# FFN up-projection on Trainium2: ten seven-product channel pairs per layer instead of seven, in groups of three

## The reference

```python
D_MODEL = 1024
SEQ = 512
D_FF = 2816
CONV_WIDTH = 3
...
def conv_ffn(x, w_up, conv_w, conv_b, w_down):
    h = x @ w_up
    ch = h.shape[-1]
    h = lax.conv_general_dilated(h, conv_w[:, None, :], window_strides=(1,), padding=((CONV_WIDTH - 1, 0),), dimension_numbers=('NWC', 'WIO', 'NWC'), feature_group_count=ch) + conv_b
    gate, val = jnp.split(h, 2, axis=-1)
    return (jax.nn.silu(gate) * val) @ w_down
...
        x = x + rms_norm(conv_ffn(rms_norm(x, pre_ffn), *ffns[i]), post_ffn)
```

## Time and profile before

| | |
|---|---|
| median of 3 runs | 2040.71 us (2038.3 to 2041.9) |
| the profiled execution | 2042.29 us, of which 2040.6 us are the span |
| PE busy | 2026.4 us (99%) |
| DVE, ACT, POOL busy | 79%, 55%, 21% |
| instructions | 33333 |
| PE clock granted | full throughout |

### The profile page before, as it was taken

One profiled execution on the slowest core, in us unless ns is written; L12 is line 12 of the kernel. 1 busy time (PEld: TensorE's weight loads), 2 busy tenths in 40 slices (PEclk: granted clock), 3 DMA queues, 4 the chain that ended last, 5 costly groups with the idle time before them and its releaser, 6 DMA issues.

```text
span 2040.6 us, 33333 instructions
## 1 busy us (share of the span) xinstructions
PE 2026.4 (99%) x12636; PEld 1750.7 (86%) x12636; DVE 1619.3 (79%) x2555; ACT 1115.0 (55%) x1861; POOL 433.7 (21%) x482
## 2 busy tenths in 40 slices
PE   9999999999999999999999999999999999999998
PEld 8889998888988899888877888998888889999887
DVE  6668878889467887899888669777997668877898
ACT  4755545447335555546656646555465755545555
POOL 0520332210000232120035402322110520332220
PEclk9999999999999999999999999999999999999999
DMA  8123344384432334467421123334674122334393
GB/s 291 64 104 125 109 130 150 121 255 172 145 129 75 97 105 129 145 190 243 166 73 42 63 83 104 119 104 155 197 237 163 65 104 83 109 122 147 115 269 122
DMA packets 82570, 276.42 MB, mean 135 GB/s; under 512 B 9408, under 2 KB 13632, under 8 KB 82032
## 3 DMA queue, kind: packets, MB, share of 16 engines
q1 hardware_dynamic: 59184, 214.67, 30.4%
q0 software_dynamic: 11200, 24.12, 5.8%
q10 hardware_dynamic: 12032, 35.54, 4.8%
HBM read 256.43 MB, written 14.73 MB: 133 GB/s over the span
## 4 chain that ended last, share of the span: by engine, by line
PE 91%; DVE 5%; DMA 2%; ACT 1%; issue 0%; DVEq 0%; ACTq 0%; SPq 0%
PE ps L2437 12%; PE ps L2438 12%; PE ps L2439 12%; PE ps L2649 6%; PE ps L3018 5%; PE ps L3019 5%; PE ps L3020 5%; PE ps L2976 5%; PE ps L2978 5%; PE ps L2977 5%; PE ps L2509 2%; PE ps L2465 2%; PE ps L2466 2%; PE ps L2467 2%; DMA raw<-slabs 2%; PE ps L2497 1%
## 5 line engine op out<-in xcount | busy, mean ns | idle before, releaser
L2437 PE MATMUL ps<-h_hi,w_hi 128*128 128x512 f32 (+1 forms) x1104 | 433.0, 392 | 0.0
L2438 PE MATMUL ps<-h_lo,w_hi 128*128 128x512 f32 (+1 forms) x1104 | 429.6, 389 | 0.0
L2439 PE MATMUL ps<-h_hi,w_lo 128*128 128x512 f32 (+1 forms) x1104 | 428.9, 389 | 0.0
L1603 DVE TENSOR_TENSOR w_lo<-raw,w_hi 128x1024 fp32r<-128x1024 f32 x300 | 372.0, 1247 | 39.1 <-ACT w_hi L901 35.5
L901 ACT ACTIVATE w_hi<-raw 128x1024 fp32r<-128x1024 f32 x312 | 326.4, 1053 | 133.1 <-DVE raw L2251 74.0
L2437 PEld LDWEIGHTS ps<-h_hi,w_hi 128*128 128x128 f32 x1104 | 207.6, 188 | 44.0 <-issue 4.0
L2439 PEld LDWEIGHTS ps<-h_hi,w_lo 128*128 128x128 f32 x1104 | 207.3, 188 | 43.2
L2438 PEld LDWEIGHTS ps<-h_lo,w_hi 128*128 128x128 f32 x1104 | 207.7, 188 | 38.9
L1281 ACT ACTIVATE work<-ps,conv_sb 128x512 f32<-128x512 f32 x120 | 93.0, 775 | 162.6 <-PE ps L2439 133.2
L3018 PE MATMUL ps<-w_hi,h_hi 128*128 128x512 f32 x408 | 159.7, 391 | 2.1 <-DVE w_lo L1603 2.1
L3020 PE MATMUL ps<-w_hi,h_lo 128*128 128x512 f32 x408 | 158.8, 389 | 0.0
(11 more groups left out here) (365 smaller groups left out, 5054.6 us busy)
## 6 DMA issues: line engine op xcount, KB each, us to landing
raw<-slabs SPq DMA_DIRECT2D x368, 512.0 KB, 4.1
act<-slabs POOLq DMA_DIRECT2D x64, 256.0 KB, 5.6
bias<-slabs SPq DMA_DIRECT2D x16, 512.0 KB, 6.3
x_dram<-x ACTq DMA_DIRECT2D x16, 512.0 KB, 5.0
x<-x_dram ACTq DMA_DIRECT2D x16, 512.0 KB, 4.9
raw<-act POOLq DMA_DIRECT2D x28, 256.0 KB, 3.3
act<-slabs SPq DMA_DIRECT2D x12, 512.0 KB, 5.4
bias_dram<-bias_rows ACTq DMA_DIRECT2D x2, 2048.0 KB, 12.3
```

The costliest lines, as they stand in the source:

```text
L1603: ve.tensor_tensor(w_lo[:, c % RING, :], raw[:, raw_slot(c), :], w_hi[:, c % RING, :].bitcast(f32), ALU.subtract).then_inc(lo_made, 1)
L2437: pe.matmul(ps[:, bank, cols], hi, h_hi[:, k, cols], start=k == 0, stop=False)
L2438: pe.matmul(ps[:, bank, cols], hi, h_lo[:, k, cols], start=False, stop=False)
L2439: last = pe.matmul(ps[:, bank, cols], lo, h_hi[:, k, cols], start=False, stop=k == KT - 1)
```

## The change

Pairs 4 to 17 are now: 4 fast, 5 ordinary, then three groups that start at `f` = 6, 10 and 14: `f`, `f + 1`, `f + 2` fast and `f + 3` ordinary. That is ten fast and four ordinary pairs a layer, instead of seven and seven. Inside a group PE interleaves products of neighbouring fast pairs. PSUM is shared out in four couples of banks, so a pair takes the banks of the pair four before. The orders of ACT, DVE, POOL and SP in this stretch are written anew as `first_period`, `period` and `last_period`; one instruction becomes four at the program's start (the negated convolution taps). The arithmetic of a fast or an ordinary pair is as before.

```diff
-FASTS = (FAST_END - FAST) // 2
+FAST_RUNS = 6, 10, 14
+IN_GROUP = 3
+FAST_PAIRS = [FAST] + [q + e for q in FAST_RUNS for e in range(IN_GROUP)]
+FASTS = len(FAST_PAIRS)
+X1_ORDER = [FAST] + [q + e for q in FAST_RUNS for e in (1, 0, 2)]
+UP_PRODUCTS = [(FAST, p) for p in (1, 2, 6, 4, 3)] + [
+    (q + e, p) for q in FAST_RUNS for e, p in (
+        (0, 1), (0, 2), (0, 6), (1, 1), (1, 2), (0, 4), (0, 3), (1, 6), (2, 1), (1, 4), (2, 2), (1, 3), (2, 6),
+        (2, 4), (2, 3))]
...
+        def part_count(L, q, name):
+
+            return FASTS * L + (X1_ORDER if name == "x1" else FAST_PAIRS).index(q) + 1
+
+        def product_count(L, q, p):
+
+            return len(UP_PRODUCTS) * L + UP_PRODUCTS.index((q, p)) + 1
...
-            return (0 if q // 2 % 2 else 4) + e
+            return 2 * ((q + 2) % 4 if FAST <= q < FAST_END else q % 2) + e
...
+                def load(q, e):
+
+                    c = up_slab(L, q, e)
+                    if q - 2 not in FAST_PAIRS:
+                        sp.wait_ge(lo_made, made(c - RAW))
+                    elif e:
+                        sp.wait_ge(part_lo_made["x3"], part_count(L, q - 2, "x3"))
+                        sp.wait_ge(part_lo_made["x4"], part_count(L, q - 2, "x4"))
+                    else:
+                        sp.wait_ge(part_lo_made["x1"], part_count(L, q - 2, "x1"))
+                        sp.wait_ge(up_x2, fast(L, q - 2) + 1)
+                        sp.wait_ge(up_x3, fast(L, q - 2) + 1)
+                    sp.dma_start(raw[:, raw_slot(c), :], slabs[dram(c)]).then_inc(raw_in[raw_slot(c)], 16)
+
+                def load_pair(q):
+
+                    load(q, 0)
+                    load(q, 1)
+
+                load_pair(FAST)
+                load_pair(FAST + 1)
+                for f in FAST_RUNS:
+                    load(f, 0)
+                    load(f + 1, 0)
+                    load(f, 1)
+                    load(f + 1, 1)
+                    load(f + 2, 0)
+                    load(f + 2, 1)
+                    load(f + 3, 0)
+                    load(f + 3, 1)
+                load_pair(FAST_END)
...
-                fourth_sum(L, FAST)
-                for j in range(STEPS - 1):
+                fourth_sum(L, 4)
+                fourth_sum(L, 6)
+                fourth_sum(L, 7)
+                down_sums(L, 0)
+                fourth_sum(L, 8)
+                down_sums(L, 1)
+                down_sums(L, 2)
+                fourth_sum(L, 10)
+                fourth_sum(L, 11)
+                fourth_sum(L, 12)
+                down_sums(L, 3)
+                down_sums(L, 4)
+                fourth_sum(L, 14)
+                down_sums(L, 5)
+                fourth_sum(L, 15)
+                fourth_sum(L, 16)
+                down_sums(L, 6)
+                for j in range(7, STEPS - 1):
                     down_sums(L, j)
-                    if FAST <= 2 * j + 4 < FAST_END and j:
-                        fourth_sum(L, 2 * j + 4)
                 first_sums(L)
...
+                if isinstance(i, int) and in_fast(c - RING):
+                    L, q, e = in_fast(c - RING)
+                    sc.wait_ge(up_mm, product_count(L, q, 2 if e else 3))
...
+                def first_period(f):
+
+                    part_hi(f, "x3")
+                    split_hi(up_slab(L, f + 1))
+                    copy(f, 0)
+                    slab_tap(f - 1, 1)
+                    slab_silu(f - 1)
+                    copy(f, 1)
+                    part_hi(f, "x4")
+                    copy(f, 2)
...
+                    copy(f + 3, 1)
...
+                def period(f):
+
+                    slab_tap(f, 0)
+                    slab_silu(f - 1)
+                    part_hi(f + 1, "x4")
+                    copy(f + 1, 2)
...
+                def last_period(f):
+
+                    slab_tap(f, 0)
+                    part_hi(f + 1, "x4")
+                    copy(f + 1, 2)
+                    part_hi(f + 2, "x1")
+                    slab_silu(f - 1)
+                    part_hi(f + 2, "x2")
+                    copy(f + 2, 0)
+                    part_hi(f + 2, "x3")
+                    split_hi(up_slab(L, f + 3))
+                    copy(f + 2, 1)
+                    s1(L, 0)
+                    s1(L, 1)
+                    s1(L, 2)
+                    slab_tap(f, 1)
+                    part_hi(f + 2, "x4")
+                    s1(L, 3)
+                    s1(L, 4)
+                    slab_tap(f + 1, 0)
...
+                def last_period(f):
+
+                    c12(f)
+                    slab_tap(f - 1, 1, 1)
+                    part_lo(f + 1, "x3")
+                    part_lo(f + 2, "a11")
+                    c11(f + 1)
+                    c22(f + 1)
+                    x2(f + 2)
+                    slab_tap(f - 1, 1, 0)
+                    x3(f + 2)
+                    part_lo(f + 1, "x4")
+                    slab_tap(f, 0, 1)
+                    part_lo(f + 2, "x2")
+                    part_lo(f + 2, "x1")
+                    part_lo(f + 2, "x3")
+                    c12(f + 1)
...
+                def bank_free(q):
+                    if q >= FAST + 2:
+                        pe.wait_ge(tap0, UP_SLABS * L + 2 * q - 6)
+
+                def p1(q):
+                    bank_free(q)
+                    pe.wait_ge(part_lo_made["a11"], part_count(L, q, "a11"))
                     product(q, 0, 0, "a11", h_quarter(0, 0), True).then_inc(up_mm, 1)
+
+                def p2(q):
                     product(q, 1, 0, "a12", h_quarter(1, 0), True).then_inc(up_mm, 1)
-                    pe.wait_ge(up_copy, 3 * f + 1)
-                    pe.wait_ge(part_lo_made["x2"], f + 1)
+
+                def p6_p5(q):
+                    pe.wait_ge(up_copy, 3 * fast(L, q) + 1)
+                    pe.wait_ge(part_lo_made["x2"], part_count(L, q, "x2"))
                     pe.wait_ge(in_lo, 4 * L + 4)
                     product(q, 0, 0, "x2", in_parts(2), False, True).then_inc(up_mm, 1)
-                    pe.wait_ge(part_lo_made["x1"], f + 1)
+                    pe.wait_ge(part_lo_made["x1"], part_count(L, q, "x1"))
                     product(q, 1, 1, "x1", in_parts(0), True).then_inc(w_used, 1)
-                    pe.wait_ge(up_copy, 3 * f + 2)
-                    pe.wait_ge(part_lo_made["x3"], f + 1)
+
+                def p7(q):
+                    pe.wait_ge(up_copy, 3 * fast(L, q) + 2)
+                    pe.wait_ge(part_lo_made["x3"], part_count(L, q, "x3"))
                     product(q, 0, 0, "x3", in_parts(1), False, True).then_inc(w_used, 1)
-                    pe.wait_ge(tap0, UP_SLABS * L + 2 * q)
-                    forward(even + 2, 0, 2)
-                    pe.wait_ge(up_c, 3 * f + 2)
+
+                def p4_p3(q):
+                    pe.wait_ge(up_c, 3 * fast(L, q) + 2)
                     product(q, 0, 0, "a22", in_parts(3), False, True).then_inc(up_mm, 1)
-                    pe.wait_ge(part_lo_made["x4"], f + 1)
+                    pe.wait_ge(part_lo_made["x4"], part_count(L, q, "x4"))
                     product(q, 1, 1, "x4", h_quarter(1, 1), False, True).then_inc(up_mm, 1)
-                    forward(even + 3, 0, 3)
+
+                p1(FAST)
+                p2(FAST)
+                p6_p5(FAST)
+                p7(FAST)
+                bank_free(FAST + 1)
+                forward(up_slab(L, FAST + 1), 0, up_bank(FAST + 1, 0))
+                p4_p3(FAST)
+                forward(up_slab(L, FAST + 1, 1), 0, up_bank(FAST + 1, 1))
+                for f in FAST_RUNS:
+                    p1(f)
+                    p2(f)
+                    p6_p5(f)
+                    p1(f + 1)
+                    p7(f)
+                    p2(f + 1)
+                    p4_p3(f)
+                    p6_p5(f + 1)
+                    p7(f + 1)
+                    p1(f + 2)
+                    p4_p3(f + 1)
+                    p2(f + 2)
+                    p6_p5(f + 2)
+                    p7(f + 2)
+                    bank_free(f + 3)
+                    forward(up_slab(L, f + 3), 0, up_bank(f + 3, 0))
+                    p4_p3(f + 2)
+                    forward(up_slab(L, f + 3, 1), 0, up_bank(f + 3, 1))
                 for q in range(FAST_END, FFT):
-                    pe.wait_ge(tap0, UP_SLABS * L + 2 * q - 2)
+                    if q < FAST_END + 2:
+                        bank_free(q)
+                    else:
+                        pe.wait_ge(tap0, UP_SLABS * L + 2 * q - 2)
                     forward(up_slab(L, q), 0, 2 * (q % 2))
```

More of the change, by code:

```diff
@@ L1321, in part_hi @@
                         sc.wait_ge(up_x2, fast(L, q) + 1)
[L1322 to L1323 removed]
+                        if before:
+                            sc.wait_ge(up_mm, product_count(L, before, 6))
                         else:
@@ L1401, in ffn_up @@
                 part_hi(FAST, "x2")
-                tap(1, 1, 0)
-                for q in range(FAST, FAST_END, 2):
-                    period(q)
-                tap(1, end - 2, 1)
```

(11 more changed lines are left out.)

390 lines of the change are left out of this document (262 added, 128 removed).

## The result

The changed kernel takes 2073.69 us (median; 2071.1 to 2078.64) against 2040.49 for the kernel before on the same chip: ratio 1.0166, 95% interval 1.0149 to 1.0182. It is 33.2 us slower. I had forecast 2038.2, in a range that ended at 2044.0. The profiled execution has a span of 2073.1 us, where before's had 2040.6: 32.5 us to be found.

What follows compares the result with a forecast made beforehand. PE's issue rate was taken as the bound. 2042.3 - 10.0 (fewer matmuls) + 7.0 (two stalls) + 0.5 (behind the stretch) = 2039.8 for the profiled execution; median 2038.2 us, range 2032 to 2044.

Steps and rivals of the forecast that it cites:

- The fewer matmuls: PE in pairs 4 to 17: more fast pairs save 2.5 us a layer, 10.0 us in four, if PE never waits.
- rival C: Narrow hand-offs to PE in the groups miss by 0.1 to 0.15 us each: 2041.8 to 2043.6 us; chance 0.14.
- (a): Start of the stretch: p6 of pair 4 waits for copy(4, 0) behind a slab's high part on ACT, 0.94 us a layer.
- (b): Last group: p3 of pair 15 waits for x4's low part, behind c22 and others on DVE, 0.82 us a layer.
- Rival B: The stalls (a) and (b) are not there, one or both: 2034.7 or 2031.2 us; chance 0.27.
- rival D: DVE, its sums stretched 0.53 us each beside POOL, becomes the bound: about 2049 to 2059 us; chance 0.07.
- six x1: DVE's x1 sums in the earlier stretch: beside POOL they lost 1.0 us in 147, taken as evidence against rival D.
- everything closes: In period, the middle groups' order, hand-offs reach PE in time; the narrow ones have 0.15 to 0.3 us to spare.
- the rule I had quoted: Two-SBUF-input VectorE and SBUF-reading GpSimd instructions exclude each other; taken at its word, low parts and sums beside POOL stretch.
- Behind the stretch: After pair 18's first forward, DVE's lateness may reach PE's longest down-projection wait: 0.5 us taken, between -1 and 2.
- 1.1 us of lateness: What remains of DVE's later finish at pair 18 after its 2.05 us of idle time takes up most.

Runs made afterwards that it cites:

- the last kernel: Changed kernel with down_sums cut to 8 columns, copy(f, 0) ahead of the slab's high part and x4's low part ahead of c22: 2032.54 us, ratio 0.9955.
- the kernel with both: Changed kernel with copy(f, 0) ahead of the slab's high part on ACT and x4's low part ahead of c22 on DVE: 2064.88 us, ratio 1.0128.
- small sums: Changed kernel with POOL's down_sums cut from 256 columns to 8, most of their sums left out: 2039.46 us, ratio 0.9995.
- POOL's new order: Changed kernel with some down_sums moved so that none lies beside x3 of pairs 8 and 12, nothing left out: 2045.27 us, ratio 1.003.
- half the width: Changed kernel with down_sums on 128 of 256 columns, half of each sum left out: 2041.81 us, ratio 1.0003.
- the two kernels with both moves and all sums: Changed kernel with copy(f, 0) and x4's low part moved earlier: 2064.88 us; the same with down_sums also moved away from x3: 2037.58 us.

## Why the prediction was wrong

**The fewer matmuls, 10.0 us: right.** 10.1, as the last kernel shows. The interleaved products run at 0.120 us a matmul, and the narrow hand-offs (rival C) don't miss.

**(a) 0.94 us a layer: right.** 0.95, in each layer. ACT at pair 4 after, to set beside the earlier trace rows, and PE:

```profile
207.34 1.04 ACT L955 ACTIVATE w_hi<-raw 128x1024 fp32r<-128x1024 f32 x1
208.29 0.36 ACT L1362 ACTIVATE bias<-ps 128x256 f32<-128x256 f32 x1
...
208.70 0.39 PE L3242 MATMUL ps<-work_r,a_hi 128*128 128x256 f32 x1 [0.79 <-ACT bias L1362]
```

**(b) 0.82 us a layer: right in kind, 0.15 too large.** It is 0.67. `c22` starts at 333.42, the low part of x4 at 335.62, 2.20 later, where I had 2.29. Both moves take their waits away, as the kernel with both shows. Rival B falls.

**DVE and POOL: the step that failed.** The prediction's sum has no term for DVE's rows beside POOL. In rival D it put 0.53 us on a sum stretched there, from one row, took the average of six x1 as evidence that even this is rare, and gave D 0.07. What it put at nothing cost 4.3 + 9.8 + 8.6 = 22.7 us in waits ahead of p4 and p6, and 4.5 more by the clock. The result lies in D's range, though not by D's mechanism: DVE never set the pace, as D says it would. There are two errors in the step.

The *size*: the x1 of the earlier trace rows met the chain of `down_sums` in its middle, 0.03 us behind the start of one POOL instruction, and waited for that one. Met at the chain's beginning, behind a `fourth_sum`, a DVE instruction can be held for the four POOL instructions together: 3.62 - 0.68 = 2.94 us. In layers 1 to 3 it is 2.96, and in layer 3 at pair 12 a 1024-wide low part takes 3.90 instead of 1.22. The earlier trace rows could not show that, since in the kernel before all chains but the first of a layer start 7 us or more behind the last `fourth_sum`. The change put three a layer straight behind one, beside a DVE row that PE needs soon, in the lines of POOL's order that stand in the diff; the prediction counted POOL's instructions and not their new neighbours. The kernel before with only these two swapped has the hold at once.

The first chain of a layer stood straight behind a `fourth_sum` in the kernel before already, and there the hold goes the other way. DVE and POOL, before, at pair 4:

```profile
205.96 0.69 DVE L2064 TENSOR_TENSOR a_lo<-act,a_hi 128x512 fp32r<-128x512 f32 x1
206.56 0.68 DVE L2078 TENSOR_TENSOR raw<-act,raw 128x512 f32<-128x512 f32 x1
...
206.26 1.59 POOL L831 TENSOR_TENSOR bias<-act 128x256 f32<-128x256 f32 x1
```

x3 has its usual 0.68 us, and POOL's first sum, which takes 0.74 alone, ends 0.61 us behind x3 (1.65 us in layers 1 to 3). So a chain straight behind an issue doesn't always hold DVE.

The *measure*: rival D asked whether DVE, on average over a group, falls behind PE, and needed seven stretched instructions. DVE never did fall behind: over the stretch it is busy 136.51 of 152.57 us, 11.4 us more than with small sums, and with POOL's new order 5.8 of these remain at no cost to PE. What counts is the room at one place. Ahead of p6 of pair 8 it is 0.98 us (with small sums x2's low part is written at 247.33 + 0.68 = 248.01, so that PE could go at 248.12, and p6 starts at its turn, 249.10). The hold of 2.94 and the 0.53 of the low part behind it make 3.47; less 0.98 that is 2.49, and PE waits 2.45. The prediction says of `period` only that everything closes; it gives the room of the narrow hand-offs and of x4's low part, but not that of x2's low part ahead of p6, and it sets no long row of DVE against any of them. The same bill fits elsewhere. With half the width 0.9 us of holds against 0.98 of room make no wait, and 1.3 us make one of 0.27 and 0.25. At pair 12 of the changed kernel the holds are 2.5 us in layer 2 and 3.2 in layer 3, and PE waits 1.52 and 2.19.

The Trainium skill (SBUF — State Buffer, "Who interferes with whom") is the rule I had quoted and given little weight: a VectorE instruction with two SBUF inputs and a GpSimd instruction that reads SBUF exclude each other. The traces now agree with it: x3, the low parts and x1 (two inputs in SBUF) are stretched, up to 3.90 us; adds in PSUM, with one, aren't (`c12` beside a chain, in the kernel before with the sums later: 0.42). What it says of the length, one instruction of the other engine, doesn't match what was measured here: the hold of x3 spans four, and that of POOL's first sum in the kernel before outlasts one DVE instruction and the next. The measurement decides.

**Behind the stretch, 0.5 us with 2 at most: wrong.** 7.0 us lie outside the stretches. PE's waits of 0.3 us and more in the down-projection add up to 8.5 us, against 2.4 before (1.48 at the place of the earlier trace rows, 0.90 in layer 1): at 440.60 1.16, at 453.57 1.95, then 0.40, 0.35, 0.94, 1.78, 0.87, 0.69 and 0.33. That explains about 6 of the 7. (The prediction's 1.1 us of lateness is 12.1 - 9.1 - 2.05 = 0.95 by its own figures; nothing hangs on the difference.) In the two kernels with both moves and all sums what lies outside the stretches is 0.9 and 1.2 us more than before, and with small sums and moves 0.1; in single executions of the other versions of the changed kernel it ranges from 0.7 to 4.9. These don't follow DVE's lateness in the stretch: POOL's new order, with no long wait in the stretch, has 4.7 us outside, and the two moves, with eight, have 1.2. Which load or low part sets each of these waits, and how much of the 7.0 belongs to the change at all, stays open.

**The clock: not in the prediction at all.** It took 2.4 GHz throughout, as before had it. Three falls cost 4.5 us; they came at waits that the holds made.

## What to carry over

When a change reorders a queue, look at what each of its instructions will now stand beside on the other engines, not at how many there are; a VectorE instruction with two inputs in SBUF beside GpSimd instructions that read SBUF is the first pair to look for. Write down for each hand-off how much room it has, and set the longest delay that could fall there against it: a queue at 90% has plenty of room on average and 1 us in the one place that matters. And a long wait can cost more than its length, if the clock falls behind it.
